# The last two output tiles of the feed-forward in token halves, with four weight pieces kept, in a two-layer encoder kernel on one NeuronCore

## What is computed

```python
for l in range(DEPTH):                       # 2 layers
    h = rms_norm(x, ln_pre_mix[l])
    m = hybrid_mixer(h, w_in[l], ...)        # its first product: h @ a 416-column slice of w_in
    x = x + rms_norm(m, ln_post_mix[l])
    h = rms_norm(x, ln_pre_ffn[l])
    gu = h @ ffn_w_gu[l]
    f = (silu(gu[..., :D_FF]) * gu[..., D_FF:]) @ ffn_w_down[l]    # D_FF = 2816, out 1024
    x = x + rms_norm(f, ln_post_ffn[l])      # needs the mean square of all 1024 columns of a token
```

## Time and profile before

| | before |
|---|---|
| median of 3 runs | 1697.42 us (1696.83 to 1698.2) |
| the profiled execution | 1697.18 us, its span 1695.4 us |
| PE busy | 1665.8 us, 98% of the span |
| POOL busy | 1095.0 us, 65% |
| DVE, ACT busy | 830.2 us (49%), 465.8 us (27%) |
| mean granted TensorE clock | 0.997 |
| DMA | 151.40 MB, mean 89 GB/s |

### The profile page before, as it was taken

One profiled execution on the slowest core, in us unless ns is written; L12 is line 12 of the kernel. 1 busy time (PEld: TensorE's weight loads), 2 busy tenths in 40 slices (PEclk: granted clock), 3 DMA queues, 4 the chain that ended last, 5 costly groups with the idle time before them and its releaser, 6 DMA issues. The chain is left out here.

```text
span 1695.4 us, 22074 instructions
## 1 busy us (share of the span) xinstructions
PE 1665.8 (98%) x8582; PEld 1397.8 (82%) x8582; DVE 830.2 (49%) x1488; ACT 465.8 (27%) x1063; POOL 1095.0 (65%) x1211
## 2 busy tenths in 40 slices
PE   7999999999999999999999999999999999999997
PEld 6888788877898888888987887988779988888886
DVE  6654558665556444410266545686564564443002
ACT  3451422434251111100155415134342411111000
POOL 8636457553669777677685365564546797776774
PEclk9999999999999999999999999999999999999999
DMA  5213222221222222222242131222112222222222
GB/s 217 75 50 112 82 81 75 75 75 50 100 76 100 100 100 100 84 87 102 95 139 75 50 120 55 100 75 75 55 70 79 97 99 100 100 99 77 101 87 84
DMA packets 27335, 151.40 MB, mean 89 GB/s; under 512 B 3483, under 2 KB 6811, under 8 KB 13376
## 3 DMA queue, kind: packets, MB, share of 16 engines
q1 hardware_dynamic: 22928, 140.70, 23.2%
q10 hardware_dynamic: 4304, 9.30, 1.8%
HBM read 147.88 MB, written 4.70 MB: 90 GB/s over the span
## 5 line engine op out<-in xcount | busy, mean ns | idle before, releaser
L561 POOL TENSOR_SCALAR w_hi<-raw 128x512 fp32r<-128x512 f32 (+3 forms) x576 | 367.1, 647 | 576.0 <-DMA raw<-stream 576.0
L565 POOL TENSOR_TENSOR w_lo<-raw,w_hi 128x512 fp32r<-128x512 f32 (+3 forms) x576 | 710.4, 1244 | 0.0
L613 PE MATMUL work<-h_hi,w_hi 128*128 128x512 f32 (+1 forms) x576 | 218.5, 379 | 1.3 <-DVE h_lo L1445 1.0
L614 PE MATMUL work<-h_lo,w_hi 128*128 128x512 f32 (+1 forms) x576 | 217.3, 377 | 0.0
L615 PE MATMUL work<-h_hi,w_lo 128*128 128x512 f32 (+1 forms) x576 | 217.3, 377 | 0.0
L738 PE MATMUL main<-h_hi,w_hi 128*128 128x512 f32 x512 | 208.3, 407 | 0.0
L738 PE MATMUL main<-h_lo,w_hi 128*128 128x512 f32 x512 | 207.1, 404 | 0.0
L738 PE MATMUL main<-h_hi,w_lo 128*128 128x512 f32 x512 | 205.4, 401 | 0.0
L613 PE MATMUL work<-act_hi,w_hi 128*128 128x512 f32 (+1 forms) x396 | 145.0, 366 | 0.0
L614 PE MATMUL work<-act_lo,w_hi 128*128 128x512 f32 (+1 forms) x396 | 144.7, 365 | 0.0
L615 PE MATMUL work<-act_hi,w_lo 128*128 128x512 f32 (+1 forms) x396 | 144.7, 365 | 0.0
(11 more groups left out here) (334 smaller groups left out, 3242.9 us busy)
## 6 DMA issues: line engine op xcount, KB each, us to landing
raw<-stream SPq DMA_DIRECT2D x106, 1024.0 KB, 4.8
raw<-stream SPq DMA_DIRECT2D x32, 704.0 KB, 4.0
raw<-stream SPq DMA_DIRECT2D x4, 832.0 KB, 4.5
x<-x_in ACTq DMA_DIRECT2D x4, 512.0 KB, 11.7
t_line<-t_first ACTq DMA_DIRECT2D x2, 1024.0 KB
rpb<-rpb_line ACTq DMA_DIRECT2D x32, 64.0 KB, 3.0
bias_b<-t_line ACTq DMA_DIRECT2D x2, 768.0 KB, 4.4
out<-x SPq DMA_DIRECT2D x6, 256.0 KB, 2.2
```

The source lines that it names most:

```text
L561: pool.tensor_scalar(w_hi[:, slot, parts[q]], raw[:, slot, parts[q]], 1.0, 0.0, ALU.mult, ALU.add).then_inc(piece_hi, 1)
L565: e = pool.tensor_tensor(w_lo[:, slot, part], raw[:, slot, part], w_hi[:, slot, part].bitcast(F32), ALU.subtract)
L613: pe.matmul(dst, a_hi, b_hi, start=first, stop=False, **kw)
L614: pe.matmul(dst, a_hi, b_lo, start=False, stop=False, **kw)
```

## The change

The last two output tiles of the feed-forward, 6 and 7, are made by token halves: tile 6 and tile 7 for tokens 0 to 255, then both for tokens 256 to 511. So the four pieces `down60`, `down61`, `down70` and `down71` are all read twice, and all must stay until their second reading. Three lie in the slots; the fourth, `down71` (`LAST_PIECE`), gets room of its own, `extra_raw`, `extra_hi` and `extra_lo`, where the attention values and the feed-forward's temporaries lie at other times. SP issues its load as soon as the feed-forward's activations are done and `down60` is split. The pieces that follow in the next layer wait for the later last readings. `mean_square` and `spread` of the first half stand at the first of the second-half entries (`m == KD`); `spread` of the second half moves ahead, from behind k = 7 of the first half's product to behind k = 6. ACT's `keep` of the two second-half entries stands behind tiles 1 and 4 of the first half's `next_input`.

```diff
-DOWN_TILES = [(d, slice(0, S)) for d in range(KD - 1)] + [(KD - 1, half) for half in HALVES]
+DOWN_TILES = [(d, slice(0, S)) for d in range(KD - 2)] + [(d, half) for half in HALVES for d in (KD - 2, KD - 1)]
+LAST_PIECE = NP_ - 1
...
+    extra_raw = sb("extra_raw", [P, 1408], F32, V)
+    extra_lo = sb("extra_lo", [P, 1408], F32R, V)
+    extra_hi = sb("extra_hi", [P, 1408], F32R, V + 5632)
...
-                    sp.wait_ge(main_done, at(l, N_MAIN, DOWNM0 + int(name[4]) + (int(name[4]) == KD - 1) + 2))
+                    sp.wait_ge(main_done, at(l, N_MAIN, DOWNM0 + int(name[4]) + 2 * (int(name[4]) >= KD - 2) + 2))
...
+                    slot = n % SLOTS
+                    if n == LAST_PIECE:
+
+                        sp.wait_ge(lo_done, at(l, N_SPLIT, ACT0 + KF))
+                        sp.wait_ge(piece_split, at(l, NP_, LAST_PIECE - SLOTS + 1))
+                        sp.dma_start(extra_raw[:, :], stream[l * NP_ + n, :, 0:size]).then_inc(piece_in[slot], 16)
+                        continue
                     if n >= SLOTS:
                         wait_freed(l, n - SLOTS)
+                    elif l and n == SLOTS - 1:
+                        sp.wait_ge(piece_split, l * NP_)
+                        wait_freed(l - 1, LAST_PIECE - SLOTS)
                     elif l:
                         wait_freed(l - 1, NP_ + n - SLOTS)
...
+                whole, high, low = raw[:, slot, :], w_hi[:, slot, :], w_lo[:, slot, :]
+                if n == LAST_PIECE:
+                    whole, high, low = extra_raw, extra_hi, extra_lo
...
                     if l and half:
-                        spread(l - 1, "post_ffn", 1)
                         pe.wait_ge(kept_done, l * N_KEPT)
...
+                        if l and half == 0 and k == 6:
+                            spread(l - 1, "post_ffn", 1)
...
-                    if ks[-1] == KH - 1 and (s or m != KD - 1):
+                    if ks[-1] == KH - 1 and (s or m not in (KD - 2, KD - 1)):
                         mm.then_inc(main_done if s else down_half, 1)
...
-                    if m < KD:
+                    if m != KD:
                         down_part(m, 0)
...
-                        if half == 0 and d == 2:
-                            keep(l, "post_ffn", KD)
+                        if half == 0 and d in (1, 4):
+                            keep(l, "post_ffn", KD + d // 4)
...
-                    if half == 0 and name == "post_ffn" and d == 4:
+                    if half == 0 and name == "post_ffn" and d == 2:
+                        sum_square(l, name, KD)
+                    if half == 0 and name == "post_ffn" and d == 5:
                         token_factor(l, name, 1)
```

More of the change, by code:

```diff
@@ L128 @@
 N_KEPT = len(OUT_TILES) + len(DOWN_TILES)
-SUMMED = [("post_mix", m) for m in range(len(OUT_TILES)) if m not in (KD - 1, len(OUT_TILES) - 1)] + [("post_ffn", m) for m in range(KD - 1)]
+SUMMED = [("post_mix", m) for m in range(len(OUT_TILES)) if m not in (KD - 1, len(OUT_TILES) - 1)] + [("post_ffn", m) for m in range(len(DOWN_TILES)) if m not in (KD - 1, len(DOWN_TILES) - 1)]
 SUMMED_AT = {n: i for i, n in enumerate(SUMMED)}
@@ L521, in wait_freed @@
                 else:
-                    sp.wait_ge(main_done, at(l, N_MAIN, DOWNM0 + int(name[4]) + (int(name[4]) == KD - 1) + 2))
+                    sp.wait_ge(main_done, at(l, N_MAIN, DOWNM0 + int(name[4]) + 2 * (int(name[4]) >= KD - 2) + 2))
             for l in range(L):
                 for n, (name, size) in enumerate(PIECES):
+                    slot = n % SLOTS
[4 more added lines that the diff above has]
+                        continue
                     if n >= SLOTS:
                         wait_freed(l, n - SLOTS)
+                    elif l and n == SLOTS - 1:
+                        sp.wait_ge(piece_split, l * NP_)
+                        wait_freed(l - 1, LAST_PIECE - SLOTS)
                     elif l:
                         wait_freed(l - 1, NP_ + n - SLOTS)
-                    slot = n % SLOTS
                     sp.dma_start(raw[:, slot, 0:size], stream[l * NP_ + n, :, 0:size]).then_inc(piece_in[slot], 16)
@@ L560, in split @@
                     if q < QUARTERS:
-                        pool.tensor_scalar(w_hi[:, slot, parts[q]], raw[:, slot, parts[q]], 1.0, 0.0, ALU.mult, ALU.add).then_inc(piece_hi, 1)
+                        pool.tensor_scalar(high[:, parts[q]], whole[:, parts[q]], 1.0, 0.0, ALU.mult, ALU.add).then_inc(piece_hi, 1)
                     if q:
@@ L564, in split @@
                         pool.wait_ge(piece_hi, at(l, QUARTERS * NP_, n * QUARTERS + q))
-                        e = pool.tensor_tensor(w_lo[:, slot, part], raw[:, slot, part], w_hi[:, slot, part].bitcast(F32), ALU.subtract)
+                        e = pool.tensor_tensor(low[:, part], whole[:, part], high[:, part].bitcast(F32), ALU.subtract)
                 e.then_inc(piece_split, 1)
@@ L1102, in down_part @@
                             wait_split(l, ("act", kk))
-                        mm = three(work[m % 2][:, cols], w_hi[:, slot, P * k:P * k + P], w_lo[:, slot, P * k:P * k + P],
+                        high, low = (extra_hi, extra_lo) if (d, s) == (KD - 1, 1) else (w_hi[:, slot, :], w_lo[:, slot, :])
+                        mm = three(work[m % 2][:, cols], high[:, P * k:P * k + P], low[:, P * k:P * k + P],
                                    act_hi[:, kk, cols], act_lo[:, kk, cols], kk == 0, kk == KF - 1)
-                    if ks[-1] == KH - 1 and (s or m != KD - 1):
+                    if ks[-1] == KH - 1 and (s or m not in (KD - 2, KD - 1)):
                         mm.then_inc(main_done if s else down_half, 1)
@@ L1409, in _ @@
                     keep(l, "post_ffn", KD)
+                    keep(l, "post_ffn", KD + 1)
                     for i, d in enumerate(range(0, LAST_GROUP, 2)):
@@ L1569, in last_output @@
                 cols = HALVES[half]
-                dve.wait_ge(kept_done, l * N_KEPT + len(OUT_TILES) + KD + half)
+                dve.wait_ge(kept_done, l * N_KEPT + len(OUT_TILES) + KD + 2 * half)
                 r = view(factor(l, "post_ffn", half), [[0, LAST_GROUP], [1, S // 2]])
@@ L1947, in _ @@
                     last_output(l, 0)
+                    sum_square(l, "post_ffn", KD)
                     token_factor(l, "post_ffn", 1)
```

## The result

The changed kernel took 1709.06 us (median, 1708.12 to 1714.95), where the kernel before, measured beside it, took 1697.21 us (1696.83 to 1698.2). The ratio is 1.0077, with a 95% interval from 1.0057 to 1.0097: slower by 11.85 us, where 11.3 were forecast. The profiled execution took 1708.92 us, its span 1706.9; its time is 11.74 us more than that of the profiled execution of before.

A forecast was written before the change was run, and what follows sets the result against it. PE, busy for 98% of the span, was taken to bound the kernel. The passage's 6.86 us (containing layer 0's 4.43) plus layer 1's 4.43 made 11.3 us: 1708.7 us as a median, range 1705.7 to 1713.5.

The forecast's parts named there:

- More matmuls: Tile 6 as two half entries on PE: 15.82 us instead of 14.96, 0.86 us more per layer.
- The other figure in the prediction: The Trainium skill's lower estimate for the two half entries of tile 6: 0.17 us more per layer.
- The wait for `down70`: Start of tile 7's first half, each layer: PE waits 2.04 us for the split of `down70`, ending at 823.87.
- The wait for `down71`: Inside tile 7's first half, each layer: PE waits 1.53 us more, for POOL's split of `down71`.
- the second rival: Slower still: half clock behind PE's new waits costs up to 1.7 us per layer, 1712.1 us; chance 0.15.
- Layer 1, +4.43 us: End of layer 1: extra matmuls and waits for `down70` and `down71` add 4.43 us; the tail is unchanged.
- The passage, +6.86 us: Between the layers: late `Dlat0` and `Dlat1` splits delay POOL's sums; +6.86 us, containing layer 0's 4.43.
- A wait of `input_square` of 1.2 us: Start of layer 1: PE is ready at 877.7 and waits about 1.2 us for POOL's sums.
- The stretch of 13.84 us: Start of layer 1, PE's road from the spread to the first gate step: 13.84 us, as in the trace.
- The rival of the clock: Half clock behind PE's new waits, uncovered behind the second: up to 1.7 us per layer, 1712.1 us; chance 0.15.
- Loads that share: Two loads issued together slow the first, `down70`: 0.7 us in each layer, 1710.1 us; chance 0.08.
- The faster rival: Tile 7's pieces ready in time: waits of 1.16 and 2.62 us between layers go, 1695.4 us; chance 0.03.

The follow-up runs named there:

- experiment 1: The changed kernel, but VectorE instead of POOL makes the low parts of `down70` and `down71` in both layers: 1702.92 us, ratio 1.0028.
- experiment 5: The changed kernel with VectorE making the low parts of `down70`, `down71`, `Dlat0`, `Dlat1`, and layer 1's start reordered on VectorE, TensorE and ScalarE: 1700.0 us, ratio 1.001.
- experiment 6: The kernel of experiment 5 with three of POOL's sums moved between the splits of `Dlat0` and `Dlat1`: 1697.93 us, ratio 0.9999.
- Experiment 7: The changed kernel with the second half's `spread` put back behind k = 7: 1711.07 us, ratio 1.0079.
- Experiment 2: The changed kernel, but VectorE instead of POOL makes the low parts of layer 1's `Dlat0` and `Dlat1`: 1708.28 us, ratio 1.0064.
- experiment 4: The kernel before with tile 6 also in token halves, each tile's halves one behind the other, no fourth piece kept: 1707.67 us, ratio 1.0056.
- 3: The changed kernel, but VectorE makes the low parts of `down70`, `down71`, `Dlat0` and `Dlat1`: 1700.17 us, ratio 1.0014.

## Why the prediction was right

The forecast was 1708.7 us, the median 1709.06. That the two lie 0.4 us apart is luck, with runs between 1708.12 and 1714.95; the waits came where the prediction put them, and in sum at its price. By its steps:

- **More matmuls, +0.86 us in each layer.** Measured 0.89 (experiment 1), 0.91 and 0.88 (5, 6), in layer 1, with no wait in it. The other figure in the prediction, 0.17 us by the Trainium skill (TensorE: Matmul & The Clock Gate, Back-to-back issue gap), rests on a formula that this section gives for an isolated matmul only, and it is not borne out by these runs; here the row and the runs agree.
- **The wait for `down70`, 2.04 us.** 2.11 us in layer 0 and 2.09 in layer 1. The split ends 10.0 us behind tile 6's start (824.46 - 814.43), where the prediction had 9.95. Its last pair of operations took 1.99 us, between the 1.86 and 2.29 of the earlier trace rows, as chosen.
- **The wait for `down71`, 1.53 us.** 1.16 us in layer 0. The first half of tile 7 nevertheless ended 11.66 us behind that of tile 6 (834.19 - 822.53), where 11.47 were forecast. The list counts a wait from the end of the last matmul, 0.16 us behind the start that a next one would have had (they start every 0.12 us and take 0.28); PE also starts a little behind POOL's end, and its first matmul takes longer (0.36 and 0.39 us). In layer 1 no second wait is listed; the clock fell to 0.50 behind the first one, the matmuls with `down70` took longer, and the entry ended 11.73 us behind the first, as in layer 0. That is what the second rival said: behind the first wait, the wait for `down71` hides it. Experiment 7 has the same in layer 0: the clock at 0.50 behind the wait for `down70`, and the entry 11.74 us long.
- **Layer 1, +4.43 us.** 4.69.
- **The passage, +6.86 us.** 6.94. `Dlat0` was waited for 2.80 us (2.9 forecast), `Dlat1`'s split began right behind its own, and POOL ran without a gap to the sums. Experiment 2 supports this chain: with the low parts of both taken from POOL, the passage is 3.31 us shorter, and no wait for the sums is left.
- **A wait of `input_square` of 1.2 us.** 0.59. This is the one term that was off by half. PE's own road was 0.6 us longer than worked out: the clock fell behind the `Dlat0` wait too (rows below), and PE came to k = 4 at 860.78, 0.8 us behind the split of `Dlat1`, where the prediction let it start at once. The sums hid that. The stretch of 13.84 us from the spread to the first gate step was right by luck. In the trace of before it held the slow clock of the earlier trace rows; in the change the clock was 1.00 there, and the stretch still took 13.53 us (864.22 to 877.75), because `h` tiles come from VectorE every 1.37 us and PE's steps kept that pace (868.51, 869.88, 871.25) where six matmuls take 1.13.
- **The rival of the clock, up to 1.7 us in each layer.** The two stretches that fell were both covered. In the change (columns as above):

```profile
826.00:829.00 3.00, 2.78 (x24) 2.58 (x22) 0.00 (x0) 0.00 (x0) 3.00 (x6) 1.00 0.00 0
831.00:834.00 3.00, 3.00 (x28) 3.00 (x27) 0.00 (x0) 0.00 (x0) 0.00 (x0) 1.00 0.03 5
...
854.00:856.00 2.00, 2.00 (x6) 1.92 (x7) 0.00 (x0) 0.00 (x0) 2.00 (x4) 0.50 0.08 27
...
1670.00:1672.00 2.00, 2.00 (x11) 2.00 (x11) 0.00 (x0) 0.00 (x0) 2.00 (x3) 0.50 0.00 0
```

  At 2.4 GHz behind the waits of 2.11 and 1.16 us, at 1.2 GHz behind those of 2.80 and 2.09: the same wait of 2.1 us had it both ways. Where nothing covers such a stretch it does cost, as experiment 5 shows.
- **Loads that share, 0.7 us in each layer.** `down70` landed after 4.2 us in layer 0 and 4.1 in layer 1, against 4.0 in the earlier trace rows.
- **The faster rival, 1695.4 us.** It hung on the split of `down70`, and the prediction's reason against it (four pieces cannot be made on POOL in the time) is what experiment 1 removes. But experiment 6, with all these waits for POOL covered, still reaches 1697.93: the rival's gain of 3.78 us was too large, since PE then waits on VectorE in three places (0.75, 0.42 and 0.75 us), and the passage gains 1.15, where 3.78 less 0.86 for its half entries would be 2.92.

## What to carry to other kernels

Before work is cut finer or reordered on the busiest engine, ask for each input when the new order wants it, and compare that with the chain that delivers it: the slot freed, the transfer, the preparation. Here four pieces at 5.49 us each stood against 15.8 us of matmuls. That rate is not all of it. POOL idled 1.88 us for `down70`'s transfer and 17.73 us for `Dlat0`'s, whose slot the second halves held longer. By an estimate from the rows, with `down70` landed 1.88 us earlier its split would have ended at 822.6, about when PE wanted it (822.3), and only the wait for `down71`, about 1.4 us, would have been left at tile 7; no run tried this. And when a feeder is relieved, list what was queued behind it: the gain passes from one wait to the next, here from the splits to VectorE's tiles and factor, then to the sums and to VectorE's low parts, and only a part of it arrives.

## What the runs showed of the hardware that was not expected

- **Late landings.** `down70`, 704 KB, landed after 4.0 to 4.3 us in the other profiled executions, but in layer 1 after 5.5 (experiment 4), 5.7 (2) and 5.9 us (3). Experiment 4 issues no second load with it, so the pair is not needed for it; what is, stays open, and with one trace of each kernel so does how often it happens. With no cover left at that place, such a landing reaches the time.
- **The clock behind short waits.** It fell behind waits of 1.03 us (experiment 5), 1.83 (4) and 2.09, and stayed up behind 1.16, 2.11 and even 3.16 (experiment 4). The same place goes both ways: behind the wait for `down70` in layer 0 it stayed up in the change (2.11 us) and fell in experiment 7 (2.09), and behind the wait for `Dlat0` it fell in the change (2.80) and stayed up in experiment 7 (2.83). In rows like these the length of a wait alone does not tell which it will be. Where nothing covered it, one slow stretch cost 1.4 us (the middle of experiment 5 against that of 6).
